# A one-core kernel for a hybrid block with experts: hx kept in SBUF through the scan, the gate in sixteen units, expert weights in 8 KB runs

## The chip, the cores and the metric

The kernel runs on one core of one Trainium2 chip. The metric is the device time in microseconds of one launch, as the median of several runs. All arithmetic is in float32.

## The reference, cut to what matters

```python
# first block: x (1, 1024, 1024), ctx (1, 256, 1024), one layer
sh_a, sc_a, g_a, sh_f, sc_f, g_f = split(silu(c) @ w_mod + b_mod, 6)
hc = ctx * (1.0 + mod_c[1]) + mod_c[0]
hx = x * (1.0 + sc_a) + sh_a
x  = layer_norm(alpha * x + g_a * latent_mixer(hx, ...), ln1_g, ln1_b)
x  = layer_norm(alpha * x + g_f * hier_moe(x * (1.0 + sc_f) + sh_f), ln2_g, ln2_b)

# latent_mixer: proj = hx @ w_in gives z, q, xbc, dt, k, v
y_f, y_b = ssd_bidirectional(xs, Bm, Cm, dt, A, hf_ctx, hb_ctx)   # chunked scan, both directions
y  = (y_f + flip(y_b) + xs * skip) * silu(z)
yg = y.reshape(L, 2, 512)                                         # two groups of 512 columns
yg = yg * rsqrt(mean(yg * yg, -1) + 1e-6)                         # a norm for each group
y_ssd = yg.reshape(L, 1024) * ssd_norm_g
# q, k: RMS norm per head, rotation; attention over 256 + 1024 keys
out = concat([y_ssd, o], -1) @ w_out

# hier_moe: 4 groups x 4 experts, 2 experts for a token; d 1024, expert width 256
gate, up = t @ w_gate[e], t @ w_up[e]
hid = silu(gate) * up * combine
y  += hid @ w_down[e]
```

A second block follows (a pooling mixer, an S5 mixer, and a feed-forward network of width 2816 made of seven half-size products). The change doesn't touch it.

## The kernel before, in words

All work is ordered by hand. Each engine has one program (a list of stage functions at the end of `build`), and semaphores tie them together; `after(eng, "ssd")` waits for all counts that end a stage. The stages of the first block are: conditions (`mod`), the modulated inputs (`hx`), the conv inputs (`xbc`), `dt`, the scan (`ssd`), the `gate`, `qkv`, the second half of the conditions (`mod2`), attention (`att`), the output product (`out`), the router and the expert slots (`moe`).

SBUF is a handful of arenas that the stages share, and `ring`, three slots of 4096 elements per partition. A panel is 1024 rows by 512 columns of a weight matrix (2 MB, in runs of 2 KB); panel j goes to slot j % 3, and `load_panels` on SP's queue waits for `panel_free[j - 3]` before it issues the load (lines 187 to 191). The panels in order are four of the conditions (0 to 3), three of xbc (4 to 6), two of z (`J_Z` = 7, 8), one of k and v (`J_KV` = 9), two of q (10, 11), then the second conditions and the output weights.

`hx`, the modulated and transposed input (8 blocks of 128 columns by 1024 tokens, 4 MB), lies in arena_b. `hc`, the same of the context (1 MB), lies in arena_t. The scan needs both places: its scratch (`xw`, `rr`, `em`, `cbm`, `tmp`, lines 216 to 221) is in arena_b, its states are over hc. So `sp_first` stores hx and hc to DRAM once they are made (lines 260, 261), the scan waits for that (`s_spill`, 32), and `sp_gate` loads them again when the scan has ended (lines 852, 853). Both z panels are loaded in the meantime.

The gate (lines 846 to 929) goes over 8 tiles of 128 tokens and two halves n of 512 columns. TensorE makes z (8 matmuls of 512 columns a unit, which the chip runs as 16 instructions), ACT takes Silu of it, VectorE multiplies it onto y, ACT squares and sums. When all 16 sums are there, one root and one reciprocal are made for all, VectorE scales the 16 pieces of y, and then TensorE transposes them, four blocks a piece, and VectorE copies each piece with its gain to `mixl`. The k, v and q products (`pe_qkv`, line 952) start after the whole gate: 10 jobs of 8 matmuls, then 8 jobs of 16, each followed by the transposes of the job before.

The experts are computed in 31 slots of 128 rows (line 1630 on). A slot's rows come from DRAM in token order of the expert (`xsl`), are transposed on TensorE (`turn`, 8 transposes, line 1648), scaled and shifted by ACT and VectorE from PSUM (`modulate`, half each, with columns of `modc`), multiplied with the gate and up weights of the slot's expert (line 1658: 8 matmuls over 512 columns, 256 of gate and 256 of up), made into hidden rows, transposed (`hidden_turn`, line 1667) and multiplied with the down weights (line 1677). TensorE's order is gate_up(s+1), hidden_turn(s), turn(s+2), down(s). The weights are double buffered. SP issues for slot s: gate and up when gate_up(s-2) has ended, then down when down(s-2) has ended; since SP's queue is in order, gate and up of slot s stand behind the wait of the down weights of slot s-1, for down(s-3). Gate and up come as `"e (k p) f -> e p k f"`, a partition reading 8 rows of 1 KB that lie 128 rows apart, down as `"e (f p) n -> e p f n"`, two rows of 4 KB. VectorE also builds tables of the second block (`dve_s5_...`) in slots 1, 3, 5, 7, 9 and 11, between `hidden_copy(s)` and `hidden(s + 1)`.

In the second block, line 1925 multiplies `hn[:, k, t:L:TC]` (TC = 8) as TensorE's weights, and line 1943 one with its weights in sequence.

Of the kernel before, what the change touches and what calls it, by code (L numbers as in the profile page):

```python
# [12 lines left out]
P = 128  # L13
D = 1024
# [63 lines left out]
def build(nc, io, out):  # L78
    ctx = ExitStack()
    with ctx:  # L80
# [25 lines left out]
        csil = sb("csil", [P, KT, 2])  # L106
        ps = ctx.enter_context(nc.psum_tensor("ps", [P, 8, HALF], F32))
# [146 lines left out]
        def sp_first(eng):  # L254
# [5 lines left out]
            eng.dma_start(hx_dram, hx.rearrange("p k n -> p (k n)")).then_inc(s_spill, 16)  # L260
# [3 lines left out]
            load_panels(eng, J_XBC + 3, J_KV)  # L264
# [350 lines left out]
        def dve_ssd(eng):  # L615
            ch = Chain(eng, steps, chained[0])
            after(eng, "xbc", "dt")
            eng.wait_ge(s_spill, 32)
# [59 lines left out]
        def pool_ssd(eng):  # L678
            after(eng, "xbc", "dt")
            eng.wait_ge(s_spill, 32)  # L680
# [36 lines left out]
        def act_ssd(eng):  # L717
            after(eng, "xbc", "dt")
            eng.wait_ge(s_spill, 32)
# [115 lines left out]
        zs = [view(arena_d, i * DSSD, DSSD) for i in range(2)]  # L835
# [3 lines left out]
        ropes = sb("ropes", [P, 2, LT, HD // 2])  # L839
# [5 lines left out]
        panel_free[J_Z] = panel_free[J_Z + 1] = (s_z, 2 * LT)  # L845

        def sp_gate(eng):
            for a in range(2):
                eng.dma_start(ropes[:, a], io["rope_table"][a].rearrange("(t p) c -> p t c", p=P)
                              ).then_inc(s_rope, 16)  # L850
            after(eng, "ssd")
            eng.dma_start(hx.rearrange("p k n -> p (k n)"), hx_dram).then_inc(s_spill, 16)
            eng.dma_start(hc.rearrange("p k n -> p (k n)"), hc_dram).then_inc(s_spill, 16)
            load_panels(eng, J_KV, NPAN1)

        def pe_gate(eng):
            after(eng, "ssd")
            eng.wait_ge(s_spill, 32 + 32)
            wait_panel(eng, J_Z)
            wait_panel(eng, J_Z + 1)  # L860
            for t in range(LT):
                for n in range(2):
                    if t >= 2:
                        eng.wait_ge(s_zs, 2 * (t - 2) + n + 1)
                    for k in range(KT):
                        mm = eng.matmul(ps[:, 2 * (t % 2) + n, :], h_tile(k, t), slot(J_Z + n)[:, k, :],  # L866
                                        start=(k == 0), stop=(k == KT - 1))
                    mm.then_inc(s_z, 1)
            eng.wait_ge(s_zn, 2 * LT)
            for t in range(LT):  # L870
                for q in range(2):
                    u = 2 * t + q
                    if u >= 4:
                        eng.wait_ge(s_zTc, u - 3)
                    for i in range(4):
                        mm = eng.transpose(ps[:, 4 + u % 4, i * P:(i + 1) * P],
                                           y[:, t, (4 * q + i) * P:(4 * q + i + 1) * P], ident[:, :])
                    mm.then_inc(s_zT, 1)

        def act_gate(eng):  # L880
            after(eng, "ssd")
            for t in range(LT):
                if t >= 2:
                    eng.wait_ge(s_zg, 2 * (t - 1))
                for n in range(2):
                    eng.wait_ge(s_z, 2 * t + n + 1)
                    eng.activation(zs[t % 2][:, n * HALF:(n + 1) * HALF], ps[:, 2 * (t % 2) + n, :], ACT.Silu
                                   ).then_inc(s_zs, 1)
# [2172 lines left out]
```

## Time and profile before

| | us |
|---|---|
| median of 3 runs | 3605.3 |
| the runs | 3598.89 to 3613.4 |
| the profiled execution | 3616.49 |
| its span (first to last instruction) | 3614.8 |
| TensorE busy | 3173.4 (88%) |
| VectorE busy | 1529.8 (42%) |
| GpSimd busy | 1051.6 (29%) |
| ACT busy | 673.3 (19%) |
| moved by DMA | 288.29 MB |

The profiled execution is one run of its own, 11 us over the median. Durations come from it. Times in the trace count from the start of its span. "PEld" is TensorE's weight load, which can overlap the matmul before it; a matmul's own duration (592 ns for 512 columns) is longer than the step from one to the next (0.43 us), since matmuls are pipelined. "issue" means that an engine waited for nothing that the profile shows.

### The profile page before, as it was taken

The page shows a single profiled execution, that of the slowest core. Times are in us where ns is not written, and L with a number is a line of the kernel's source. Part 1 is how long each engine was busy: PE and PEld are TensorE (multiplying, and loading weights), DVE is VectorE, ACT ScalarE, POOL GpSimd, SP SyncE. Part 2 cuts the span into 40 slices and gives each one's busy share as a digit, 9 for nine tenths or more (in the row PEclk, how much of TensorE's full clock was granted, in tenths as well). Part 3 has the DMA queues.
Part 4 walks back from the last instruction along what each step waited for, and adds up shares of the span by engine and source line. Part 5 has one row for each costly group of instructions (what it writes and reads, how often), then busy time and mean ns, then how long its engine had stood idle before and what let it go on. Part 6 is the DMA issues. An engine that isn't in the chain of part 4 may idle for free.

```text
span 3614.8 us, 27752 instructions
## 1 busy us (share of the span) xinstructions
PE 3173.4 (88%) x9880; PEld 1480.6 (41%) x9880; DVE 1529.8 (42%) x2447; ACT 673.3 (19%) x1440; POOL 1051.6 (29%) x953
## 2 busy tenths in 40 slices
PE   6996879898999999999758999198698999999995
PEld 3553434443333333344424444165444444444442
DVE  2335851444555555422323322616413343454345
ACT  1224631111222222300111111212201000000001
POOL 0004840000365656600010000214401355345534
PEclk8998989998999999999879999598799999999998
DMA  7000020104600000010188998300102011111101
GB/s 283 24 26 1 1 82 0 47 24 168 245 1 1 1 1 1 5 61 18 38 299 283 320 332 286 142 4 12 47 0 70 23 61 45 35 35 65 40 12 53
DMA packets 170617, 288.29 MB, mean 80 GB/s; under 512 B 22216, under 2 KB 108912, under 8 KB 169968
## 3 DMA queue, kind: packets, MB, share of 16 engines
q1 hardware_dynamic: 155632, 237.02, 19.0%
q10 hardware_dynamic: 10240, 32.71, 2.4%
q0 software_dynamic: 4608, 16.78, 1.2%
q8 instruction: 79, 1.29, 0.1%
q14 instruction: 58, 0.48, 0.0%
HBM read 236.17 MB, written 50.33 MB: 79 GB/s over the span
## 4 chain that ended last, share of the span: by engine, by line
PE 63%; issue 13%; POOL 9%; DVE 7%; DMA 6%; ACT 2%; SPq 0%; ACTq 0%; POOLq 0%; DVEq 0%
PE ps L2792 15%; PE ps L2808 6%; PE ps L1329 6%; PE ps L422 6%; PE ps L967 5%; POOL arena_b L1205 5%; PE ps L1658 5%; PE ps L2597 3%; PE ps L866 3%; DMA ring<-in_w_up 3%; PE ps L1677 2%; PE ps L1925 2%; PE ps L1943 2%; DMA ring<-in_w_mod 1%; PE ps L1107 1%
## 5 line engine op out<-in xcount | busy, mean ns | idle before, releaser
L1205 POOL TENSOR_TENSOR arena_b<-arena_b 128x512 f32<-128x512 f32 x288 | 357.6, 1268 | 298.6 <-ACT arena_b L1187 298.6
L1223 DVE TENSOR_REDUCE arena_b<-ps 128x1 f32<-128x512 f32 (+1 forms) x384 | 213.0, 597 | 245.6 <-PE ps L1107 244.4
L2764 POOL TENSOR_TENSOR arena_b<-arena_b,arena_d 128x512 f32<-128x512 f32 x132 | 165.8, 1272 | 374.4 <-DVE arena_d L2899 372.8
L1658 PE MATMUL ps<-ring,arena_a 128*128 128x512 f32 x496 | 235.5, 631 | 36.7 <-issue 16.4
L2877 DVE TENSOR_TENSOR arena_d<-arena_d,ps 128x512 f32<-128x512 f32 x154 | 101.8, 684 | 385.8 <-PE ps L2792 385.8
L1187 ACT ACTIVATE arena_b<-ps 128x512 f32<-128x512 f32 x320 | 173.7, 594 | 416.1 <-PE ps L1133 416.1
L1107 PE MATMUL ps<-arena_d,arena_a 64*128 64x512 f32 (+1 forms) x768 | 243.0, 575 | 2.3 <-DVE arena_b L1214 2.1
L1129 PE MATMUL ps<-arena_a,arena_d 64*128 64x512 f32 x640 | 218.2, 617 | 8.3 <-DVE arena_b L1243 8.3
L2896 DVE TENSOR_TENSOR arena_b<-arena_b,ps 128x512 f32<-128x512 f32 x264 | 174.6, 685 | 49.3 <-POOL arena_b L2764 25.9
L1143 PE MATMUL ps<-arena_b,arena_d 128*64 128x512 f32 x640 | 172.7, 617 | 0.0
L967 PE MATMUL ps<-ring,arena_b 128*128 128x512 f32 x384 | 169.1, 597 | 1.7 <-DVE arena_c L924 1.7
L1658 PEld LDWEIGHTS ps<-ring,arena_a 128*128 128x128 f32 x496 | 98.7, 202 | 169.7 <-issue 144.9
L422 PE MATMUL ps<-arena_b,ring 128*128 128x512 f32 x384 | 166.9, 592 | 0.8 <-ACT arena_b L401 0.8
L1107 PEld LDWEIGHTS ps<-arena_d,arena_a 64*128 64x128 f32 x768 | 86.0, 189 | 182.9 <-issue 119.0
L2792 PE MATMUL ps<-arena_a,ring 128*128 128x512 f32 x352 | 154.7, 598 | 1.3 <-DVE arena_a L1882 1.3
L1615 POOL DMA_INDIRECT arena_d<-yslots,arena_t x8 | 7.6, 945 | 448.4 <-DMA yslots<-arena_a 442.3
L687 POOL TENSOR_TENSOR arena_b<-m_le,arena_t 128x512 f32<-128x512 f32 x32 | 40.4, 1262 | 315.6 <-DVE arena_t L558 310.2
L2808 PE MATMUL ps<-arena_c,arena_t 128*128 128x512 f32 x264 | 128.2, 594 | 0.0
L866 PE MATMUL ps<-ring,arena_b 128*128 128x512 f32 x256 | 111.8, 599 | 15.7 <-DMA arena_t<-hc_dram 15.7
L1398 PE MATMUL ps<-ident,arena_t 128*128 128x128 f32 x128 | 26.5, 379 | 100.4 <-ACT arena_t L1821 84.3
L1677 PE MATMUL ps<-ring,arena_c 128*128 128x512 f32 x248 | 111.7, 593 | 2.0 <-DVE arena_c L1753 1.5
L1329 PE MATMUL ps<-ring,arena_c 128*128 128x512 f32 x256 | 113.2, 595 | 0.0
(504 smaller groups left out, 5006.4 us busy)
## 6 DMA issues: line engine op xcount, KB each, us to landing
ring<-in_w_gate SPq DMA_DIRECT2D x42, 1024.0 KB, 7.6
ring<-in_w_up SPq DMA_DIRECT2D x42, 1024.0 KB, 10.8
ring<-in_w_down SPq DMA_DIRECT2D x42, 1024.0 KB, 5.5
ring<-in_w_mod SPq DMA_DIRECT2D x12, 2048.0 KB, 13.3
ring<-in_w_in SPq DMA_DIRECT2D x10, 2048.0 KB, 13.2
xslots<-arena_c SPq DMA_DIRECT2D x1, 15872.0 KB, 52.1
arena_a<-xslots ACTq DMA_DIRECT2D x31, 512.0 KB, 5.6
yslots<-arena_a ACTq DMA_DIRECT2D x31, 512.0 KB, 5.4
```

What stands on the lines that cost most here:

```text
L422: mm = eng.matmul(ps[:, b, 0:n], w[:, k, (m % 4) * P:(m % 4 + 1) * P], src[:, k, :], start=(k == 0), stop=(k == KT - 1))
L866: mm = eng.matmul(ps[:, 2 * (t % 2) + n, :], h_tile(k, t), slot(J_Z + n)[:, k, :], start=(k == 0), stop=(k == KT - 1))
L967: mm = eng.matmul(ps[:, 2 * (j % 2) + n, :], h_tile(k, t), w[:, k, :], start=(k == 0), stop=(k == KT - 1))
L1107: eng.matmul(ps[:, u % 3, 0:k1 - k0], qT[rows, pr, q0:q0 + P], kT[rows, pr // 2, k0:k1], start=True, stop=True).then_inc(s_S, 1)
L1129: eng.matmul(ps[:, 4 + e, :], kT[rows, pr // 2, kt * P:(kt + 1) * P], qT[rows, pr, qs], start=True, stop=False)
L1205: eng.tensor_tensor(acc, first, prT[n % NPR], ALU.add).then_inc(s_pa, 1)
L1223: eng.tensor_reduce(mx3[j % 2][:, t, e, piece:piece + 1], ps[:, u % 3, 0:k1 - k0], AX.X, ALU.max).then_inc(s_mx, 1)
L1329: mm = eng.matmul(ps[:, u % 3, :], (mixl if k < KT else mixu)[:, k % KT, t * P:(t + 1) * P], w[:, k % KT, :], start=(k == 0), stop=(k == 2 ...
L1658: mm = eng.matmul(ps[:, s % 2, :], xsT[s % 2][:, k, :], sguw[s % 2][:, k, :], start=(k == 0), stop=(k == KT - 1))
L1677: mm = eng.matmul(ps[:, 5 + h, :], hTs[s % 2][:, f, :], sdnw[s % 2][:, f, h * HALF:(h + 1) * HALF], start=(f == 0), stop=(f == 1))
L2792: mm = eng.matmul(bank_of("gu", b, w, p), lhs, rhs, start=(k == 0), stop=(k == HK - 1))
L2808: eng.matmul(bank_of("dn", b, i, p), lhs[p], rhs[p], start=True, stop=True).then_inc(dn_done, 1)
```

## The change

1. hx stays in arena_b through the scan. The scan's scratch moves to the ring: `uu` and `rr` to slot 0, `xw`, `em` and `cbm` to slot 2; the two `tmp` rows go to the free end of arena_d and into the buffer of the rope tables. Only the first z panel (slot 1) is loaded before the scan. The second, hc and the rope tables are loaded after it. hc is still stored and loaded again.
2. The gate runs as 16 units, half n = 0 of all tiles first. Each unit has its own sum, root and reciprocal, and is transposed two units later, between the z products. The first k/v product is issued ahead of the last transposes.
3. The expert weights are read so that a partition takes 8 adjacent rows of gate and of up (8 KB in one run) and 2 adjacent rows of down (8 KB). The contraction index of block k is then p * 8 + k instead of k * 128 + p. So the transposes of the slot's rows read every 8th column, those of the hidden rows every 2nd, and the shift and scale come from a new table `modp` in that order, made by a trip of the 16 columns through DRAM behind `mod2`.

```diff
-        xw = view(arena_b, 0, 2, DSSD)
-        rr = view(arena_b, 2048, 2, 2, HALF)
-        em = view(arena_b, 4096, 2, HALF)
-        uu = view(ring, 0, 2, 2, HALF)
-        cbm = view(arena_b, 6144, 2, 2, 2 * NST)
-        tmp = [view(arena_b, 7168 + i * HALF, HALF) for i in range(2)]
-        hx_dram = nc.dram_tensor("hx_dram", [P, KT * L], F32).ap()
+        uu, rr = view(ring, 0, 2, 2, HALF), view(ring, 4 * HALF, 2, 2, HALF)
+        xw = view(ring, 2 * PAN, 2, DSSD)
+        em = view(ring, 2 * PAN + 4 * HALF, 2, HALF)
+        cbm = view(ring, 2 * PAN + 6 * HALF, 2, 2, 2 * NST)
+        tmp = [view(arena_d, 4 * (L + CTX) + NT * 2 * NST, HALF),
+               ropes[:, :, :, :].rearrange("p a t c -> p (a t c)")]
...
-            eng.dma_start(hx_dram, hx.rearrange("p k n -> p (k n)")).then_inc(s_spill, 16)
-            load_panels(eng, J_XBC + 3, J_KV)
+            load_panels(eng, J_XBC + 3, J_Z + 1)
...
         def sp_gate(eng):
+            after(eng, "ssd")
+            load_panels(eng, J_Z + 1, J_KV)
+            eng.dma_start(hc.rearrange("p k n -> p (k n)"), hc_dram).then_inc(s_spill, 16)
             for a in range(2):
                 eng.dma_start(ropes[:, a], io["rope_table"][a].rearrange("(t p) c -> p t c", p=P)
                               ).then_inc(s_rope, 16)
-            after(eng, "ssd")
-            eng.dma_start(hx.rearrange("p k n -> p (k n)"), hx_dram).then_inc(s_spill, 16)
-            eng.dma_start(hc.rearrange("p k n -> p (k n)"), hc_dram).then_inc(s_spill, 16)
             load_panels(eng, J_KV, NPAN1)
...
+            for u, (n, t) in enumerate(ZUNITS):      # pe_gate
+                if t == 0:
+                    wait_panel(eng, J_Z + n)
+                if u >= 4:
+                    eng.wait_ge(s_zs, u - 3)
+                for k in range(KT):
+                    mm = eng.matmul(ps[:, u % 4, :], hx[:, k, t * P:(t + 1) * P], slot(J_Z + n)[:, k, :],
+                                    start=(k == 0), stop=(k == KT - 1))
+                mm.then_inc(s_z, 1)
+                if u >= 2:
+                    turn(u - 2)
+            turn(2 * LT - 2)
+            pe_qkv_product(eng, 0)
+            turn(2 * LT - 1)
...
+            for u, (n, t) in enumerate(ZUNITS):      # act_gate
+                eng.wait_ge(s_z, u + 1)
+                if u >= 4:
+                    eng.wait_ge(s_zg, u - 3)
+                eng.activation(zs[u % 4], ps[:, u % 4, :], ACT.Silu).then_inc(s_zs, 1)
                 eng.wait_ge(s_zg, u + 1)
+                    eng.wait_ge(s_zss, 2 * u)
                 eng.activation(sqz, y[:, t, n * HALF:(n + 1) * HALF], ACT.Square,
                                accum_out=ssum[:, u:u + 1]).then_inc(s_zss, 1)
+                eng.wait_ge(s_zq, 2 * u + 1)
+                eng.activation(rst[:, u:u + 1], ssum[:, u:u + 1], ACT.Sqrt).then_inc(s_zss, 1)
...
+        modp = csil.rearrange("p k v -> p (k v)").rearrange("p (v k) -> p v k", v=2)
+        def sp_mod_columns(eng):                     # SP: behind sp_zero, ahead of sp_out
+            after(eng, "mod2")
+            eng.dma_start(mod_dram.rearrange("(n p) -> p n", p=P), modc[:, 3 * KT:5 * KT, 0],
+                          allow_slow_non_contiguous=True).then_inc(s_rope, 16)
+            eng.wait_ge(s_rope, 32 + 16)
+            eng.dma_start(modp, mod_dram.rearrange("(v p k) -> p v k", v=2, k=KT)).then_inc(s_rope, 16)
...
-            gate_of = io["w_gate"][0].rearrange("e (k p) f -> e p k f", p=P)
-            down_of = io["w_down"][0].rearrange("e (f p) n -> e p f n", p=P)
+            gate_of = io["w_gate"][0].rearrange("e (p k) f -> e p k f", p=P)
+            down_of = io["w_down"][0].rearrange("e (p f) n -> e p f n", p=P)
-                eng.dma_start(sguw[s % 2][:, :, 0:FE], gate_of[e]).then_inc(gu_in[s % 2], 16)
-                eng.dma_start(sguw[s % 2][:, :, FE:], up_of[e]).then_inc(gu_in[s % 2], 16)
+                eng.dma_start(sguw[s % 2][:, 0], gate_of[e]).then_inc(gu_in[s % 2], 16)
+                eng.dma_start(sguw[s % 2][:, 1], up_of[e]).then_inc(gu_in[s % 2], 16)
...
-                                       xsl[s % 3][:, k * P:(k + 1) * P], ident[:, :])
+                                       xsl[s % 3].rearrange("p (c k) -> p k c", k=KT)[:, k, :], ident[:, :])
-                    mm = eng.matmul(ps[:, s % 2, :], xsT[s % 2][:, k, :], sguw[s % 2][:, k, :],
+                    mm = eng.matmul(ps[:, s % 2, :], xsT[s % 2][:, k, :], sguw[s % 2][:, :, k, :],
-                    mm = eng.transpose(ps[:, 4, f * P:(f + 1) * P], hds[s % 2][:, f * P:(f + 1) * P], ident[:, :])
+                    mm = eng.transpose(ps[:, 4, f * P:(f + 1) * P], hds[s % 2].rearrange("p (c f) -> p f c", f=2)[:, f, :], ident[:, :])
```

## Rows read from the trace of the kernel before

**Rows 1.** The page: busy tenths of TensorE and DMA in 40 slices of 90 us.
```profile
PE   6996879898999999999758999198698999999995
DMA  7000020104600000010188998300102011111101
```
**Rows 2.** The chain of waits, 500 to 700 us: start us, us, what.
```profile
515.19 0.70 DVE arena_a L635
...
516.29 14.24 DMA arena_t<-hc_dram
...
530.88 111.78 PE ps L866 x256
...
666.98 15.70 PE ps L967 x32
...
683.12 6.87 PE ps L967 x16
```
**Rows 3.** The timeline of ACT at the gate's end: start us, us, what.
```profile
642.69 0.60 ACT L887 ACTIVATE arena_d<-ps 128x512 f32<-128x512 f32 x1 [6.21 <-PE ps L866]
643.18 0.62 ACT L901 ACTIVATE arena_d<-arena_a 128x512 f32<-128x512 f32 x1
...
643.99 0.63 ACT L901 ACTIVATE arena_d<-arena_a 128x512 f32<-128x512 f32 x1
...
646.35 1.28 ACT L893 ACT_TABLE_LOAD   x1
```
**Rows 4.** The timeline of VectorE, gate's end and first k row.
```profile
643.32 0.69 DVE L909 TENSOR_TENSOR arena_a<-arena_a,arena_d 128x512 f32<-128x512 f32 x1 [6.12 <-ACT arena_d L887]
...
680.15 0.43 DVE L1050 COPY arena_c<-arena_t 128x512 f32<-128x512 f32 x1
```
**Rows 5.** TensorE's groups, 1847 to 2256 us: busy us, mean ns, idle before.
```profile
L1658 PE MATMUL ps<-ring,arena_a 128*128 128x512 f32 x496 | 235.5, 631 | 36.7 <-issue 16.4 <-DMA ring<-in_w_up 16.2 <-ACT arena_a L1708 4.1
```
**Rows 6.** The timeline of TensorE in the slots: start us, us, what.
```profile
1963.48 0.38 PE L1667 MATMUL ps<-ident,arena_a 128*128 128x128 f32 x2
1963.70 1.04 PE L1648 MATMUL ps<-ident,arena_a 128*128 128x128 f32 x8
1964.57 3.60 PE L1677 MATMUL ps<-ring,arena_c 128*128 128x512 f32 x8
1972.52 9.86 PE L1658 MATMUL ps<-ring,arena_a 128*128 128x512 f32 x16 [4.36 <-issue]
```
**Rows 7.** The timeline of VectorE ahead of the gate/up product at 1972.5.
```profile
1971.06 1.36 DVE L1739 TENSOR_SCALAR arena_a<-ps,modc 128x128 f32<-128x128 f32 x4
```
**Rows 8.** The chain of waits, 2035 to 2068 us.
```profile
2038.09 3.45 PE ps L1677 x8
...
2043.17 11.71 DMA ring<-in_w_up
```
**Rows 9.** Line 1637, which loads w_up: its 31 DMAs.
```profile
DMA to landing us min/median/max: 9.3/11.1/32.9
```
**Rows 10.** Windows: us, PE, PEld, DVE, ACT, POOL busy, PEclk, DMA share, GB/s.
```profile
1972.00:1980.00 8.00, 7.48 (x11) 3.29 (x12) 1.55 (x3) 0.00 (x0) 0.00 (x0) 0.62 0.89 300
...
1805.00:1843.00 38.00, 0.00 (x0) 0.00 (x0) 10.91 (x49) 1.86 (x4) 15.44 (x16) 0.50 1.04 403
```
**Rows 11.** GB/s in 40 slices: runs of 1 KB (2829:2843), 2 KB (2572:2582), 4 KB (3479:3488).
```profile
GB/s 0 0 0 0 0 0 79 102 219 304 372 383 395 383 383 369 360 342 351 354 348 342 348 336 193 26 0 0 0 0 0 0 0 0 0 0 0 0 0 0
GB/s 0 0 0 0 0 131 156 180 352 336 401 410 401 401 393 377 393 418 410 410 401 418 418 401 401 401 393 336 49 0 0 0 0 0 0 0 0 0 0 0
GB/s 0 0 0 0 127 18 309 146 182 255 400 437 400 437 400 400 419 400 310 18 0 0 0 0 0 0 0 0 0 0 0 0 0 0 0 0 0 0 0 0
```
**Rows 12.** Weight loads of lines 1925 and 1943: ns min/median/max, first and last start.
```profile
L1925 PEld LDWEIGHTS ps<-ring,arena_a x128: 312/313/334, 2358.1 to 2412.4; 128*128 128x128 f32 x128
L1943 PEld LDWEIGHTS ps<-arena_a,ring x128: 190/190/192, 2412.8 to 2473.4; 128*128 128x128 f32 x128
```
**Rows 13.** The timeline of TensorE, 301.7 to 304.5 us.
```profile
301.81 2.42 PE L522 MATMUL ps<-sel,arena_a 128*128 128x32 f32 x20 [1.61 <-DVE arena_a L538]
```

More of the change, by code:

```diff
@@ L834, in build @@
         mixl = view(arena_c, 0, KT, L)
-        zs = [view(arena_d, i * DSSD, DSSD) for i in range(2)]
+        zs = [view(arena_d, i * HALF, HALF) for i in range(4)]
         sqz = view(arena_d, 2 * DSSD, HALF)
@@ L857, in pe_gate @@
             after(eng, "ssd")
[L858 to L878, printed above, removed]
+            def turn(u):
+                n, t = ZUNITS[u]
+                eng.wait_ge(s_zn, u + 1)
+                if u >= 4:
+                    eng.wait_ge(s_zTc, u - 3)
+                for i in range(4):
+                    mm = eng.transpose(ps[:, 4 + u % 4, i * P:(i + 1) * P],
+                                       y[:, t, (4 * n + i) * P:(4 * n + i + 1) * P], ident[:, :])
+                mm.then_inc(s_zT, 1)
@@ L880, in act_gate @@
+            turn(2 * LT - 2)
+            pe_qkv_product(eng, 0)
+            turn(2 * LT - 1)
         def act_gate(eng):
             after(eng, "ssd")
[L882 to L888, printed above, removed]
-                if t >= 1:
-                    gate_squares(eng, t - 1)
@@ L891, in act_gate @@
-            gate_squares(eng, LT - 1)
-            eng.wait_ge(s_zq, 1)
-            eng.activation(rst, ssum, ACT.Sqrt).then_inc(s_silu, 1)
-        def gate_squares(eng, t):
-            for n in range(2):
-                u = 2 * t + n
+            for u, (n, t) in enumerate(ZUNITS):
+                eng.wait_ge(s_z, u + 1)
+                if u >= 4:
+                    eng.wait_ge(s_zg, u - 3)
+                eng.activation(zs[u % 4], ps[:, u % 4, :], ACT.Silu).then_inc(s_zs, 1)
                 eng.wait_ge(s_zg, u + 1)
@@ new lines, in dve_gate @@
+            for u, (n, t) in enumerate(ZUNITS):
+                v = y[:, t, n * HALF:(n + 1) * HALF]
+                r = rst[:, u:u + 1]
+                eng.wait_ge(s_zs, u + 1)
+                eng.tensor_tensor(v, v, zs[u % 4], ALU.mult).then_inc(s_zg, 1)
+                if u >= 3:
+                    turned_gate(u - 3)
+                eng.wait_ge(s_zss, 2 * u + 1)
+                step(eng, eng.tensor_scalar(ssum[:, u:u + 1], ssum[:, u:u + 1], 1.0 / HALF, EPS_RMS,
+                                            ALU.mult, ALU.add), s_zq, 2 * u + 1)
+                eng.wait_ge(s_zss, 2 * u + 2)
+                step(eng, eng.reciprocal(r, r), s_zq, 2 * u + 2)
+                eng.tensor_scalar(v, v, r, None, ALU.mult).then_inc(s_zn, 1)
@@ L932, in build @@
+            for u in range(2 * LT - 3, 2 * LT):
+                turned_gate(u)
+        ends["gate"] = [(s_zTc, 2 * LT), (s_zq, 4 * LT), (s_zs, 2 * LT), (s_zss, 4 * LT)]
         kT = view(arena_d, 0, KVH, L + CTX)
@@ L950, in build, with pe_qkv_product @@
         panel_free[J_Q] = panel_free[J_Q + 1] = (s_qkp, NJ)
+        def pe_qkv_product(eng, j):
+            kind, t = JOBS[j]
+            if j == 0:
+                wait_panel(eng, J_KV)
+            if j == LT:
+                eng.wait_ge(s_spill, 16 + 16)
+            if j == NT:
+                wait_panel(eng, J_Q)
+                wait_panel(eng, J_Q + 1)
+            if j < 2:
+                eng.wait_ge(s_zs, 2 * LT - 2 + 2 * j)
+            else:
+                eng.wait_ge(s_qkn, j - 1)
+                eng.wait_ge(s_qkv, min(j - 1, NT))
+            for n in range(2 if kind == "q" else 1):
+                w = slot(J_Q + n) if kind == "q" else slot(J_KV)
+                for k in range(KT):
+                    mm = eng.matmul(ps[:, 2 * (j % 2) + n, :], h_tile(k, t), w[:, k, :],
+                                    start=(k == 0), stop=(k == KT - 1))
+            mm.then_inc(s_qkp, 1)
@@ L1586, in build @@
         BS = KT * 2 * FE + 2 * D
-        sguw = [view(ring, i * BS, KT, 2 * FE) for i in range(2)]
+        sguw = [view(ring, i * BS, 2, KT, FE) for i in range(2)]
         sdnw = [view(ring, i * BS + KT * 2 * FE, 2, D) for i in range(2)]
```

102 lines of the change are left out of this document (38 added, 64 removed).

## The prediction, made before the changed kernel was run

> **What bounds the kernel now.** I began with the page: TensorE works 88% of the span and is at 9 tenths or more of a slice nearly everywhere except around slices 6 and 7 (about 515 to 670 us) and 19 to 25 (1780 to 2300 us); DMA is near idle except in the second of these, around attention's end and at the start [rows 1]. So two stretches matter: the end of the scan with the gate behind it, and the expert slots.
>
> For the first I read the chain of waits [rows 2]. VectorE's last addition of the scan ends at 515.9, hx and hc come back from DRAM until 530.5, the 256 z matmuls (16 units of 16) take 111.8, and then a serial tail (squares, root, 16 scalings of y, 64 transposes with their copies) runs until the first k/v product at 667.0. In steady state a product takes 6.87 and 0.44 for its four transposes, without a gap (the first two end at 682.68, the next starts at 683.12). The tail is 667.0 - 642.7 = 24.3 us.
>
> For the slots I read TensorE's groups, then its timeline. Gate/up waited 36.7 us in all: 16.4 in five slots put down to "issue", 16.2 in six for w_up, 4.1 at the start for ACT [rows 5]. A slot without a wait is gate/up 6.87 (16 matmuls, as a k/v product), hidden turn 0.22, turn of x 0.87, down 3.44: 11.4 us [rows 6]. 31 of them are 353; the stretch from 1847 to 2256 has 409. The five are slots where VectorE works through s5 tables before the next hidden and modulated rows: its scaling of rows ends at 1972.4 and gate/up starts at 1972.5 [rows 6, 7]. That gate/up takes 9.86, where 16 such matmuls take 6.87 otherwise; the granted clock there is 0.62 of full [rows 6, 10]. The loads set the rest: a slot's weights are issued when the down product of three slots earlier ends, here at 2041.5, and w_up lands at 2054.9, 13.3 later, against a slot of 11.4 [rows 8]. From its own issue it takes at least 9.3 and 11.1 in the median [rows 9].
>
> **Gate.** (1) The hx reload goes: z can start at 516.1. The second z panel (2 MB) is now loaded there and needed at unit 8, 58 us on; hc and the rope tables ride behind it, needed after 640. All of that is under 4 MB, and the 5 MB of before landed in 14.2 us [rows 2]. (2) A unit becomes 6.87 + 0.44 = 7.31, the step that the k/v products already show: 16 units are 117.0. The first k/v product is issued ahead of the last turn, so the second starts at 516.1 + 117.0 + 6.9 = 640.0. Before, it starts at 682.7 - 6.9 = 675.8. Gain 35.8.
>
> What could take it back is the chain through ACT and VectorE, now serial per unit, with Silu's and Sqrt's tables alternating. By the rows [rows 3, 4]: Silu 0.63 to the multiply, multiply 0.69, Square with its accumulator read 0.81, mean 0.2, table load 1.28, the root of one column 0.3 by the size of such small steps, table load for the next Silu 1.28: 5.2 us per unit against 7.31. Both loads are counted in full, so nothing comes on top if they queue behind a wait. The cover is 2.1 us; without it each missing us costs 16. The last unit's chain (5.5 with reciprocal and scaling) lies under the turn before it and a product (7.3), and the first k row's chain (675.8 to VectorE's copy ending at 680.6, 4.8, plus 0.9 for the gate's last copy) under the second product [rows 4]. The idle 15 us before z and the tail each left a slow start (15.70 for two products instead of 13.74), which the smaller seams may keep or lose: +2 or -1. So 33.8 to 36.8, and I take 35.6.
>
> **Scan.** Its buffers move (xw, rr, em, masks to the ring, two scratch rows elsewhere); instructions, shapes and types stay. No row shows that an address matters. The 4 MB store of hx also goes; it is issued when hx is made, and the scan, which waits for it, comes only after all conv products. Nothing, +-1.
>
> **Expert weights.** (3) Gate and up come in 8 KB runs instead of 1, down in 8 instead of 4. Of three loads that run alone, 1 KB runs settle at 342 to 354 GB/s, 2 KB runs at 401 to 418, 4 KB at 400 to 437 [rows 11]. There is no 8 KB row; the nearest is 4 KB, so I take 410 (bounds 345 and 435). The 2.1 MB then take 5.1 instead of 6.0 us. All DMA work of a slot, 3.1 MB of weights and 1.05 MB of rows in and out, is 10.2 us at 410 and 12.0 at 350. (4) The rows' columns must follow the weights' new order, so the turn of x reads `xsl` at a stride of 8 elements as TensorE's weights. The trace has this access: L1925 loads `hn[:, k, t:L:TC]`, TC = 8, in 313 ns, beside 190 for the same shape in sequence in L1943 [rows 12]. There it hid under 512-column matmuls. In a turn it can't: eight turns in 0.87 are one per 0.109, and L522's 20 matmuls of 32 columns keep 0.113 too [rows 6, 13], so the pace is that of the weight loads. Plus 0.123 each, 0.98 per slot. Bounds: nothing, and 0.327 each if a strided load ran at a quarter of that pace. The hidden turn has stride 2 and no row; 0 to 0.25 per slot, and I take 0, as half of each piece read is still used.
>
> The Trainium skill ("SBUF — State Buffer", "Door 1: The DMA port swizzle") speaks against (4): accesses that each go to a new 16-byte line pay a penalty, and two hits per line are enough for full bandwidth. The trace agrees for the stride of 8 and gives the size [rows 12]; of the stride of 2 no run here shows anything yet. By that rule the sum would stay as it is.
>
> (5) A slot becomes 12.4. In the five slots bound by VectorE the longer turn lies inside the wait (2.6 to 4.4), so 26 x 0.98 = +25.5. The waits for w_up go: the work of 10.2 is under 12.4, and w_up lands 13.3 less 0.9 and less the backlog, about 11 behind the down product. That is 16.2 and the slow clock behind them, at most 3 each as at 1972.5 and less behind shorter waits; I take 4 for the six: -20 (bounds -14, if some come back, and -22). The start of the stage, 1805 to 1843, is all DMA at 403 GB/s [rows 10], 4.2 MB of it in 1 KB runs: -1.5 (0 to -2). The waits for VectorE stay.
>
> (6) The shift and scale columns go to DRAM and back in 4-byte pieces. Both DMAs and SP's wait for mod2, which ends ahead of attention, stand behind the zero fill and ahead of the out stage's loads, which wait for attention (1533) anyway; the columns are needed at 1843. Attention covers them by 600 us. Nothing. The new waits of ACT and VectorE in the slots are fulfilled long before.
>
> **Sum.** -35.6 + 25.5 - 20 - 1.5 = -31.6. The profiled execution (3616.5) goes to 3585, the median of the runs (3605.3, 11 lower) to 3574. Half a percent, about what a measurement of this kernel can tell from no change, is 18 us: faster is under 3587.
>
> **Rivals.** A, the strided turn is free, because loads overlap deeper in a turn than under a matmul. The +25.5 goes away, the slot stays 11.4 and some short waits for w_up return (+3): 3551. For it: loads of 190 ns keep a pace of 0.11 as well as those of 140. Against: 123 ns more for the same 128 columns look like time of reading. Chance 0.13.
> B, run length brings nothing in the mix of queues and 350 GB/s remains. Then 12.0 of work meets a slot of 12.4, w_up lands about 12.7 behind and 0.3 late in 24 slots, and the start gains nothing: +9, 3583. For it: beside POOL's queue 403 GB/s is reached with 1 KB runs in the mix [rows 10]. Chance 0.14.
> The Trainium skill ("DMA: Bandwidth & Descriptors", "Specifications") backs B: from 512 bytes on a transfer runs at line rate. By that rule 1 KB runs lose nothing; the rates of the loads alone, 350 beside 405, speak against it [rows 11].
> C, a gate unit's chain is longer than TensorE's 7.31, say 8.3 with VectorE's copies in the way: +16, 3590. Against: 5.2 by the rows. Chance 0.06.
> D, slower than before: strided loads at a quarter pace in both turns. Ten per slot at 0.327 are 3.3 us, in 26 slots +85 instead of +25.5: 3633. It decides from 0.22 per load on (57 us of gains / 26 / 10). Against: 0.123 by L1925. Chance 0.05.
> That the change doesn't do what it says would be a gap at 516 as before; the reload of hx is out of the code, so that gets no chance of its own. The forecast keeps 0.62.
>
> **Numbers.** 3574 by the forecast case, whose own bounds give 3560 to 3588. The range of 3550 to 3593 takes in A, B and C; D is left out. The forecast case lies nearly whole under 3587, A wholly, B for the most part, C hardly: faster 0.85, same 0.10, slower 0.05.
>
> **What the profile after should show.** z within 1 us of the scan's end; a step of 7.3 in the gate; the second k/v product at 640; ACT idle some 2 us per unit. Loads of the x turn near 260 ns, eight turns in 1.85 us; slots of 12.4 with no wait for w_up; the five s5 waits 1 us shorter, their gate/up starting as late behind the hidden turn as now. I am wrong if turns still take 0.87 (A), if w_up is waited for by more than a few us in all (B), if gate steps are over 7.5 (C), or if turns take over 3 us (D).

## The result, and the profile after

| | before | after |
|---|---|---|
| median, run side by side | 3605.56 us (4 runs) | 3569.59 us (4 runs, 3567.2 to 3576.23) |
| ratio | | 0.9894, 95% interval 0.9878 to 0.991 |
| the profiled execution, its span | 3616.49, 3614.8 | 3567.2, 3565.5 |
| TensorE busy | 3173.4 (88%) | 3159.0 (89%) |
| ACT busy | 673.3 | 715.2 |
| moved by DMA | 288.29 MB | 279.93 MB |

The median falls by 36.0 us, to 4 under the forecast of 3574. The two profiled executions differ by 49.3, because that of before was 11 over its median and that of after 2 under it.

The page after the change, against [rows 1]: a slice is now 89 us. The holes at the end of the scan and in the slots are narrower, but the second is still there (slices 19 to 25).

```profile
PE   6996889997999999999668997297698999999995
...
DMA  6000010107300000100378897100102021112101
```

The chain of waits after, 509 to 645 us, against [rows 2]: start us, us, what.

```profile
509.71 0.70 DVE arena_a L634
510.41 0.04 issue
510.45 23.20 PE ps L874 x48
533.65 0.44 PE ps L864 x4
534.09 6.87 PE ps L874 x16
540.96 0.44 PE ps L864 x4
541.40 6.87 PE ps L874 x16
...
628.63 0.87 PE ps L864 x8
629.50 6.87 PE ps L963 x16
636.37 0.44 PE ps L864 x4
636.81 6.87 PE ps L963 x16
```

No DMA stands between the scan and z. From the end of the scan (510.4) to the second k/v product (636.8) are 126.4 us, where before there were 159.9 (515.9 to 675.8): 33.5 less. A step is 7.31 (534.09 to 541.40), as forecast. Only the start is slow: the first three units take 23.2 for what later takes 20.6. Two windows of that stretch say why (us, PE, PEld, DVE, ACT, POOL busy, PEclk, DMA share, GB/s):

```profile
510.50:515.00 4.50, 4.50 (x6) 1.92 (x7) 0.00 (x0) 0.00 (x0) 0.00 (x0) 0.50 0.77 245
515.00:534.00 19.00, 19.00 (x49) 8.66 (x48) 2.99 (x8) 9.76 (x14) 0.00 (x0) 1.00 0.69 232
```

z starts at a granted clock of 0.50, the lower level of 1.2 GHz, and is at 1.00, 2.4 GHz, in the window from 515 on. The clock fell ahead of z: it is 1.00 from 503 to 508 and 0.61 from 508.0 to 509.7, where the scan's last eight small products run behind 1.75 us without work.

The timeline of ACT in a gate unit, against [rows 3]:

```profile
595.75 1.28 ACT L889 ACT_TABLE_LOAD   x1
599.45 0.60 ACT L889 ACTIVATE arena_d<-ps 128x512 f32<-128x512 f32 x1 [2.41 <-PE ps L874]
600.80 0.63 ACT L893 ACTIVATE arena_d<-arena_a 128x512 f32<-128x512 f32 x1 [0.76 <-DVE arena_a L911]
601.34 0.19 ACT L893 ACTIVATION_READ_ACCUMULATOR arena_d<-arena_a 128x1 f32 x1
601.54 1.28 ACT L896 ACT_TABLE_LOAD   x1
602.84 0.20 ACT L896 ACTIVATE arena_d<-arena_d 128x1 f32<-128x1 f32 x1
603.05 1.28 ACT L889 ACT_TABLE_LOAD   x1
```

ACT waits 2.41 us per unit for TensorE, so its chain stays under the product; the table load for the next Silu (595.75) is made ahead of that wait, not behind it.

TensorE in the slots after, as its group, then a plain stretch of its timeline, against [rows 5, 6]:

```profile
L1671 PE MATMUL ps<-ring,arena_a 128*128 128x512 f32 x496 | 231.1, 621 | 28.7 <-issue 17.4 <-DMA ring<-in_w_up 7.2 <-ACT arena_a L1721 4.1
```

```profile
1998.42 7.03 PE L1671 MATMUL ps<-ring,arena_a 128*128 128x512 f32 x16
2005.29 0.39 PE L1680 MATMUL ps<-ident,arena_a 128*128 128x128 f32 x2
2005.51 1.06 PE L1661 MATMUL ps<-ident,arena_a 128*128 128x128 f32 x8
2006.41 3.60 PE L1690 MATMUL ps<-ring,arena_c 128*128 128x512 f32 x8
2009.85 7.03 PE L1671 MATMUL ps<-ring,arena_a 128*128 128x512 f32 x16
```

A slot without a wait takes 11.43 (1998.42 to 2009.85), as before, not 12.4: the strided turn costs 0.90 (2005.51 to 2006.41) where the plain one cost 0.87. The waits for w_up are 7.2 us instead of 16.2, not gone. Those of VectorE (issue, 17.4) are there as they were.

By stage the difference between the two profiled executions (-49.3) is: scan end -5.5, gate -33.5, start of the slots (scatter to first turn) +0.8, first turn to the end of the last down product -11.6 (413.4 to 401.9), the rest within 0.5. The -5.5 isn't the change's: the conv products, whose code is the same, start at 57.2 here and at 60.6 there, and the scan's end goes with that start. The kernel before, profiled once more (`e4` below), starts them at 57.2 too and ends its scan at 510.7, beside 510.4 here; this kernel, profiled once more (`e5`), starts them at 60.9 and ends its scan at 516.9.

### The profile page after: what moved, and what is told of

Same layout as the page of the kernel before. It is cut to its first block, busy times and chain, and to the rows that moved or that the text cites. A ratio compares the mean times of both kernels' runs of the same rounds, so it can differ in the third digit from the quotient of the medians.

```text
span 3565.5 us, 27860 instructions
## 1 busy us (share of the span) xinstructions
PE 3159.0 (89%) x9880; PEld 1471.4 (41%) x9880; DVE 1535.9 (43%) x2477; ACT 715.2 (20%) x1485; POOL 1051.1 (29%) x953
## 2 busy tenths in 40 slices
DMA packets 113147, 279.93 MB, mean 79 GB/s; under 512 B 24520, under 2 KB 47728, under 8 KB 100848
## 4 chain that ended last, share of the span: by engine, by line
PE 65%; issue 13%; POOL 9%; DVE 7%; DMA 4%; ACT 1%; ACTq 0%; SPq 0%; POOLq 0%; DVEq 0%
PE ps L2807 15%; PE ps L2823 6%; PE ps L1331 6%; PE ps L421 6%; PE ps L1671 5%; PE ps L963 5%; POOL arena_b L1207 5%; PE ps L874 3%; PE ps L2612 3%; PE ps L1690 2%; DMA ring<-in_w_up 2%; PE ps L1940 2%; PE ps L1958 2%; DMA ring<-in_w_mod 1%; PE ps L1109 1%
## 5 line engine op out<-in xcount | busy, mean ns | idle before, releaser
L1671 PE MATMUL ps<-ring,arena_a 128*128 128x512 f32 x496 | 231.1, 621 | 28.7 <-issue 17.4
L686 POOL TENSOR_TENSOR ring<-m_le,arena_t 128x512 f32<-128x512 f32 x32 | 40.4, 1262 | 309.7 <-DVE arena_t L557 306.0
```

Of the source, the lines that this page charges most:

```text
L1671: mm = eng.matmul(ps[:, s % 2, :], xsT[s % 2][:, k, :], sguw[s % 2][:, :, k, :], start=(k == 0), stop=(k == KT - 1))
```

## The experiments

In all kernels the time from the start of the first gate/up product to the start of the last matmul of the last down product is called the slot stretch. It is 409.0 us in the profile of before, 397.3 in that of after. The ratios of each table are to the kernel before, run beside the kernels of that table; that is why its median differs from table to table.

### Each half of the change alone

`e1_gate_part` is the changed kernel with the expert part undone. `e2_weights_part` is the kernel before with the expert part alone. `e3_hx_reloaded` is the changed kernel with the store and reload of hx back in. `e4_before_again` is the kernel before, profiled once more.

e1 against the changed kernel (e2 has the same lines the other way, against the kernel before):

```diff
-            gate_of = io["w_gate"][0].rearrange("e (p k) f -> e p k f", p=P)
+            gate_of = io["w_gate"][0].rearrange("e (k p) f -> e p k f", p=P)
...
-                                       xsl[s % 3].rearrange("p (c k) -> p k c", k=KT)[:, k, :], ident[:, :])
+                                       xsl[s % 3][:, k * P:(k + 1) * P], ident[:, :])
```

e3 against the changed kernel:

```diff
+            eng.dma_start(hx_dram, hx.rearrange("p k n -> p (k n)")).then_inc(s_spill, 16)
...
+            eng.dma_start(hx.rearrange("p k n -> p (k n)"), hx_dram).then_inc(s_spill, 16)
```

Besides, hc's reload goes ahead of the second z panel again, and z waits for both reloads, as in the kernel before.

> The change without its expert weights: hx kept, gate in units, weights and row turns of the slots as before. Theory (the two parts are independent, gate worth 33.5 us by the traces): 3605.6 - 33.5 = 3572, ratio 0.9907; w_up waited for as often as before (about 16 us). Rival (the profiled pair differs by 49 us because the gate part is worth more than its stage, through a shift of later stages): under 3562.

> The expert weights alone on the kernel before: 8 KB runs, strided turns, the table of shifts in the new order. Theory (the traces give 413.4 to 401.9 us for the slots): -11.6, so 3594, ratio 0.9968. Rival (what the blind sum said: turns 0.98 us longer, loads hidden): +4, ratio 1.001. Rival (the medians moved by 36, the gate took 33.5 of it, so the weights are worth only 2.5): ratio 0.9993.

> The changed kernel with hx stored and reloaded as before, everything else kept (gate in units, last panel behind the reloads). Theory (the reload is the gap of 14.2 to 15 us ahead of z, of which a slow start of 1 us comes back): +14, so 3584 against 3569.6 of the change, ratio to before 0.9939. Rival (the gate in units hides part of the reload): under +5.

> The kernel before once more, for its profile alone. Theory (the first profiled execution was 11 us over the median by chance, in the waits for w_up and in the start): a span nearer 3603, the slots shorter than 413 us or the start shorter. Rival (profiling adds it always): a span near 3615 again.

Measured, against a median of 3610.69 for the kernel before (19 runs, 3597 to 3624):

| kernel | median us | ratio (95%) | z starts | slot stretch | waits for w_up | issue |
|---|---|---|---|---|---|---|
| e1, gate part | 3581.28 | 0.9924 (0.9897 to 0.995) | 516.7 | 405.9 | 12.5 | 16.3 |
| e2, weights part | 3604.62 | 0.9981 (0.9962 to 1.0) | 530.7 | 398.6 | 7.5 | 16.2 |
| e3, hx reloaded | 3589.53 | 0.9942 (0.9923 to 0.9961) | 527.0 | 397.2 | 7.4 | 17.4 |
| e4, before again | 3608.14 (one run) | | 525.8 | 403.3 | 9.8 | 16.3 |

The chain of waits of e3 behind the scan:

```profile
511.17 0.70 DVE arena_a L636
512.27 14.49 DMA arena_t<-hc_dram
527.00 18.07 PE ps L878 x38
...
652.52 6.87 PE ps L967 x16
```

The gate part brings 27 us by its ratio (18 to 37 by the interval; 33.5 by the trace), the weights part 7 (0 to 14). Their product, 0.9905, lies in the interval of the whole (0.9878 to 0.991). e1's median of 3581 is 9 over what was expected of it, with an interval that takes in the expected 0.9907; its slots waited 12.5 us for w_up.

By the traces hx in SBUF is a little less than half of the gate part. With the reloads ahead of z again, z starts 15.1 us behind VectorE's last addition instead of 0.04. From the scan's end (511.9) to the second k/v product (652.5) e3 takes 140.6 us, where the changed kernel takes 126.4 and the one before 159.9. So the reloads are 14.2 of the 33.5 and the gate in units is 19.3. The medians give the reloads more: e3 is 18 to 20 us slower than the changed kernel (3571.61 and 3569.59 in its two sets of runs), where 14 was expected. Of the 18.3 between the two profiles, 2.5 lie between the k/v products and the first slot. There two executions of the changed kernel itself (after and e5) differ by 3.1, so this part isn't shown to be the reload's.

e4 shows what one profile hides. Its w_up waits are 9.8 us and its slot stretch 403.3, where the first profile of the same kernel had 16.2 and 409.0. The old weights give 409.0, 403.3 and 405.9 (mean 406.1); the new ones, in five profiles (after, e2, e3, e5, e6), 397.2 to 398.6 (mean 397.7). So the weights part is worth 8.4 us, and some 3 of the 11.6 between the two profiles were the draw of one execution.

### The strided turn and the run length

`e5_change_again` is the changed kernel unaltered. `e6_plain_turns` reads the rows in sequence in both turns. `e7_short_runs` brings the weights in runs of 1 and 4 KB again and leaves all else. In both, the rows' columns no longer stand in the order of the weight rows, so that the expert products multiply other pairs.

e6 against the changed kernel (it is the same in the hidden turn), then e7:

```diff
-                                       xsl[s % 3].rearrange("p (c k) -> p k c", k=KT)[:, k, :], ident[:, :])
+                                       xsl[s % 3][:, k * P:(k + 1) * P], ident[:, :])
```

```diff
-            gate_of = io["w_gate"][0].rearrange("e (p k) f -> e p k f", p=P)
-            up_of = io["w_up"][0].rearrange("e (p k) f -> e p k f", p=P)
-            down_of = io["w_down"][0].rearrange("e (p f) n -> e p f n", p=P)
+            gate_of = io["w_gate"][0].rearrange("e (k p) f -> e p k f", p=P)
+            up_of = io["w_up"][0].rearrange("e (k p) f -> e p k f", p=P)
+            down_of = io["w_down"][0].rearrange("e (f p) n -> e p f n", p=P)
```

> The changed kernel again, as the base for the other kernels of this row. Theory (gate -34 by the traces, weights -8 as the mean of three profiles each way): ratio 0.988 to 0.990, slots of 397 to 399 us, six VectorE-bound waits of 16 to 18 us in all, w_up waited for 7 to 8.

> The changed kernel with the turns of x and of the hidden rows read in sequence again; this leaves the columns in another order than the weights' rows, so values differ. Theory (a strided turn costs only 0.02 us, rival A of the prediction): loads 140 instead of 193 ns, no difference in time, under 1 us. Rival (the strided turn holds something back that the turn's own time does not show, e.g. the row scaling or the DMA writes into SBUF): 5 us or more faster, slots under 393 us.

> The changed kernel with its expert weights in 1 and 4 KB runs again, turns strided; the rows of the weights are then in another order than the columns, so values differ. Theory (the gain of the weights part is run length alone): slots back to 403 to 409 us, w_up waited for 10 to 16 us, +8 on the change. Rival (the gain came from the new place or order in SBUF): slots stay at 397 to 399.

Measured, against a median of 3612.14 for the kernel before (7 runs):

| kernel | median us | ratio (95%) | slot stretch | w_up | issue |
|---|---|---|---|---|---|
| e5, change again | 3571.61 | 0.988 (0.9863 to 0.9896) | 397.9 | 7.5 | 17.4 |
| e6, plain turns | 3569.12 | 0.9877 (0.9861 to 0.9894) | 397.3 | 7.3 | 16.3 |
| e7, short runs | 3579.17 | 0.9908 (0.989 to 0.9926) | 405.3 | 15.4 | 13.6 |

The x turn's weight loads, after and in e6, then those of the hidden turn after (ns min/median/max):

```profile
L1661 PEld LDWEIGHTS ps<-ident,arena_a x248: 186/193/226, 1805.1 to 2186.5; 128*128 128x128 f32 x124
```

```profile
L1661 PEld LDWEIGHTS ps<-ident,arena_a x248: 139/140/230, 1805.7 to 2187.1; 128*128 128x128 f32 x124
```

```profile
L1680 PEld LDWEIGHTS ps<-ident,arena_a x62: 194/196/199, 1827.2 to 2201.5; 128*128 128x128 f32 x62
```

The strided load of a transposition takes 193 ns instead of 140, and the kernel doesn't feel it: e5 and e6 have the same time within their intervals and the same stretch within 0.6 us. That is rival A's outcome. A stride of 2 costs the load as much as one of 8: 196 ns, where e6 has 141. The shorter runs cost 8 us by the medians (3579.17 beside 3571.61, with intervals that just overlap), and the slots show it more clearly (405.3 beside 397.9; no profile with long runs is over 398.6), with the waits for w_up back at 15.4. The stretch 1835 to 2195 of after, then of e7, shows the same load on the queues at another price:

```profile
1835.00:2195.00 360.00, 335.39 (x958) 163.01 (x957) 118.86 (x315) 52.83 (x140) 0.00 (x0) 0.97 0.85 324
```

```profile
1835.00:2195.00 360.00, 331.00 (x941) 160.86 (x940) 116.26 (x310) 51.48 (x136) 0.00 (x0) 0.96 0.92 318
```

The DMA engines are busy 0.85 of the time for 324 GB/s, and 0.92 for 318: per byte 10% more with short runs. So run length matters and rival B falls. Whether gate and up (1 KB) or down (4 KB) bring the most wasn't told apart.

### When does a strided load cost its time?

The prediction priced the turn by a strided load of the second block (313 ns). `e8_matmul_turns` makes the x turn of the changed kernel a plain float32 product with the identity, which the chip runs as 16 instructions, with the same strided rows. `e12_matmul_in_seq` is e8 with rows in sequence; as in e6, other pairs are multiplied.

```diff
-                    mm = eng.transpose(ps[:, 2 + k // 4, (k % 4) * P:(k % 4 + 1) * P],
-                                       xsl[s % 3].rearrange("p (c k) -> p k c", k=KT)[:, k, :], ident[:, :])
+                    mm = eng.matmul(ps[:, 2 + k // 4, (k % 4) * P:(k % 4 + 1) * P],
+                                    xsl[s % 3].rearrange("p (c k) -> p k c", k=KT)[:, k, :], ident[:, :],
+                                    start=True, stop=True)
```

> The changed kernel with the turn of x done as a plain float32 product with the identity (two instructions a block) instead of a transposition. It measures the strided load as in the second block's product with hn. Theory (there a strided load reads at half pace, 313 ns, while a transposition's load is another, shorter form): loads of 313 ns and one instruction per 0.23 us, a turn of 3.7 us, slots 2.8 us longer. Rival (load time beyond the pace is latency that overlaps in either form): one per 0.11 us, a turn of 1.8 us, slots 0.9 us longer.

> The kernel of e8_matmul_turns (the x turn as a plain float32 product with the identity, 16 instructions), but with rows read in sequence instead of at a stride of 8; this makes the columns of the rows stand in another order than the weight rows, which changes that part of the computation. e8's turns hold loads of 335 ns and one instruction per 0.237 us, 3.79 to the next operation. If the stride is what costs in the plain float32 form, and only there, loads are 190 ns, as in the second block's line with weights in sequence, and the pace falls to 0.11 to 0.12: the turn takes 1.9 and the stage of 31 slots 451 - 31 x 1.9 + some waits for w_up = 395 to 405. Rival: the plain form itself is slow at 128 columns, stride or not: pace 0.237 as before, stage 451.

The timeline of TensorE in e8, then in e12:

```profile
2014.04 3.96 PE L1661 MATMUL ps<-ident,arena_a 128*128 128x128 f32 x16
2017.83 3.60 PE L1691 MATMUL ps<-ring,arena_c 128*128 128x512 f32 x8
```

```profile
2011.63 1.95 PE L1661 MATMUL ps<-ident,arena_a 128*128 128x128 f32 x16
2013.42 3.60 PE L1691 MATMUL ps<-ring,arena_c 128*128 128x512 f32 x8
```

Turn to down product is 3.79 us with strided rows, 1.79 in sequence: 0.237 and 0.112 per instruction, with loads of 335 and 192 ns. So the +0.125 is real in a plain float32 product, and there it comes with the stride alone. In a transposition the stride adds 53 ns to the load and 0.004 to the pace (0.112 beside 0.109). The single runs were 3629.72 (e8, stretch 451.2) and 3579.67 (e12, stretch 403.8). They show a second thing: with a slot of 14.3 the waits for w_up are gone, with 12.3 they are 1.7 us. The waits put down to issue fell too, to 2.4 and 12.0: a longer slot gives VectorE more time.

### What still holds the slots

The chain of waits after, in a slot that waits for w_up, against [rows 8]:

```profile
2029.43 3.45 PE ps L1690 x8
2032.89 0.33 SPq L1653
...
2033.98 1.27 SPq L1649
...
2035.35 10.58 DMA ring<-in_w_up
2045.93 0.04 issue
2045.97 7.13 PE ps L1671 x16
```

The down product's end releases SP, which issues down, gate and up in this order. w_up lands at 2045.93, 13.1 behind the product; in the next slot 11.9 (2057.69 to 2069.63). The landing alone is 10.6 and 10.4 here, and 10.0 to 12.2 in all six slots where w_up ends the chain, beside 10.9 to 13.9 in nine such slots of before [rows 8]. `e9_loads_ahead` lets SP issue gate and up ahead of the wait for the down buffer; `e10_tables_behind` moves VectorE's s5 tables behind the rows that TensorE waits for; `e11_both` does both.

e9:

```diff
-                if s >= 2:
-                    eng.wait_ge(dn_done, s - 1)
-                eng.dma_start(sdnw[s % 2], down_of[e]).then_inc(dn_in[s % 2], 16)
+                if s >= 1:
+                    down_load(s - 1)
...
+            down_load(NSLOT - 1)
```

Here `down_load(s)` holds the three removed lines for slot s. In e10 these lines of VectorE's program now stand ahead of the slot's `dve_s5_...` calls, not behind them:

```python
                 if s + 1 < NSLOT:
                     hidden(s + 1)
                 if s + 2 < NSLOT:
                     modulate(s + 2)
                 store(s)
```

> The changed kernel, with SP issuing gate and up of slot s before it waits to issue down of slot s-1; nothing else moved. If the waits for w_up that are left (7 to 9 us in the changed kernel and its repetition) come from SP standing in front of the down load while gate and up could go already, they go away: the ratio to the kernel before falls from 0.989 to 0.987, about 3562, and the stage of 31 slots from 398 us to 390. The waits put down to issue (17.4), which are VectorE's, stay. Rival: the weights' buffers are free only when their product ends, so that an earlier issue starts no earlier or meets the rows of x and y in the queues: no change, 3570.

> The changed kernel, with VectorE's s5 table work of a slot moved behind the hidden rows, the modulated rows and the store of the same slot. If the waits put down to issue are VectorE standing in the s5 tables before the rows that TensorE waits for, they go (17.4 us), with the slow clock behind them (up to 3 in each of six slots, of which I count 1 each): 20 us less, 3550, ratio 0.983, the stage 378 us. Rival: the slots without a wait run into the loads and waits for w_up grow from 7 to 15 or more, as with short runs: 12 us less or under, 3558.

> Both moves at once, in the changed kernel. If VectorE's tables and SP's order are all that holds the slots above 11.43 us, the stage of 31 slots is 31 x 11.43 + 6 = 360 us instead of 398, and the kernel 3535, ratio 0.979. Rival: the loads themselves are the bound by then (10 us of DMA work per slot, with the landing 10 to 12 after the issue), and waits for w_up of 10 us or more are left: 3550, ratio 0.983.

Measured, against a median of 3611.46 for the kernel before (7 runs):

| kernel | median us | ratio (95%) | slot stretch | w_up | issue |
|---|---|---|---|---|---|
| e9, loads ahead | 3558.93 | 0.9853 (0.9826 to 0.988) | 387.9 | 0 | 17.4 |
| e10, tables behind | 3548.37 | 0.9817 (0.9785 to 0.9849) | 375.1 | 11.9 | 0 |
| e11, both | 3534.4 | 0.9785 (0.9758 to 0.9812) | 360.8 | 0 | 0 |

TensorE's group in e10, then in e11:

```profile
L1671 PE MATMUL ps<-ring,arena_a 128*128 128x512 f32 x496 | 221.1, 599 | 16.1 <-DMA ring<-in_w_up 11.9 <-ACT arena_a L1721 4.1
```

```profile
L1677 PE MATMUL ps<-ring,arena_a 128*128 128x512 f32 x496 | 220.7, 598 | 4.1 <-ACT arena_a L1727 4.1
```

Each move takes away the wait it aims at, and the waits of the other kind stay or grow (7.2 to 11.9 in e10). The slow clock goes with VectorE's waits: behind one of them, from 1985.2 to 1990.0, the changed kernel has a granted clock of 0.64, and gate/up is busy 231.1 in it and 221.1 in e10, whose clock from 1835 to 2155 is 1.00. The stretch lost 17.4 of waits and these 10.0 (6 were counted), and got back 4.7 of waits for w_up: 22.7, about what it shows (397.3 to 375.1), where 20 was expected. With both moves the stretch is 360.8, as expected 360, and the loads are still not the bound at 11.4 us per slot, though the DMA engines are busy 0.92 of the time from 1835 to 2155. e11 is 35 us under the changed kernel (37 under e5) and 77 under the one before.

## Why the prediction was right, and where its steps were not

The range held and the gate's mechanism came as forecast, but that the time was met to 4 us is in part luck. The two largest terms of the slots were both wrong: the 25.5 us of the strided turn didn't come, and the waits for w_up gave back 11.6 less than forecast. The two errors partly cancelled.

**Gate (1, 2): forecast -35.6, measured -33.5.** The reload's place, the step of 7.31 and the cover of about 2 us on ACT came as forecast, and rival C falls. ACT's chain is 4.9 us per unit (599.45 to 604.33) where 5.2 was counted. From the scan's end to the second k/v product the forecast was 123.9 us (516.1 to 640.0) and the trace has 126.4. Nearly all of the 2.5 is the first z products at clock 0.50. The prediction had this as "+2 or -1" at the seams and took 0.2. The chain of waits in e11, at the start and the end of the gate:

```profile
515.13 0.04 issue
...
631.01 0.87 PE ps L864 x8
631.89 6.87 PE ps L963 x16
638.76 0.44 PE ps L864 x4
639.19 3.01 PE ps L963 x7
```

From 515.1 to 639.2 are 124.1, the forecast. A window of its first z products has the granted clock at 1.00:

```profile
515.30:519.80 4.50, 4.50 (x11) 2.07 (x12) 0.00 (x0) 0.00 (x0) 0.00 (x0) 1.00 0.78 246
```

The code up to there is that of the changed kernel. In e11 the clock is 1.00 in the scan's last eight products too (513.3 to 514.4), where after it had fallen. Three executions (e10, e11, e12) have no slow z product, the longest being 0.70 us; seven (after, e1, e5 to e9) have one of 1.22. Why, stays open. All three had a late start of the conv products (60.3 to 61.0), but so had e1 and e5.

**Scan: forecast nothing, +-1, and so it came.** From the first conv product to the scan's end, executions that start these products at 56.9 to 57.8 take 453.5 with the old buffers (e4) and 453.2 to 453.6 with the new ones (after, e6 to e9), with 454.4 in e3. Those that start at 60.3 to 61.0 take 455.3 and 455.0 with the old (before, e2) and 454.9 to 456.0 with the new (e1, e5, e10 to e12). The 2 us go with the start, not with the buffers. Why there are two starts is open.

**Strided turn (4, 5): forecast +25.5, measured nothing (0.03 us a slot in the timeline, none in e6).** This is the step that failed. The load of `L1925` (313 ns) is that of a plain float32 product, the turn's that of a transposition. The same stride of 8 costs 0.125 us per instruction in the one form, as computed, and 0.004 in the other. The price went wrong with the row that it was taken from. Rival A, with 0.13, named the outcome but not the reason: a load as long as that row's isn't hidden in a turn either (335 ns in e8, pace 0.237); the transposition's is a shorter one. Its time of 3551 was 18 us too low, because it too let nearly all waits for w_up go. By the prediction's own sign (turns that still take 0.87; they took 0.90) the forecast case was wrong here. What misled me was "the pace is that of the weight loads": before, loads of 140 ns and of 190 ns had the same pace of 0.11 [rows 6, 13], which already said that a load up to 190 is hidden. 193 was just inside, 335 far outside; no run has a load between them in a turn.

The Trainium skill ("SBUF — State Buffer", "Door 1: The DMA port swizzle") says that accesses to a new 16-byte line each pay a penalty and that two hits per line are enough for full bandwidth. At the stride of 8 the loads agree in direction, 193 beside 140 ns in transpositions and 335 beside 192 in plain products. At the stride of 2, which takes two float32 elements from each such line, the trace doesn't agree: 196 beside 141 ns, as much as at 8. That a longer load can be hidden whole is shown by e6.

**Waits for w_up: forecast -20, measured about -8.** This term hung on the wrong one: it let them go because a slot would be 12.4 long. With a slot of 11.43 and w_up landing 11.9 and 13.1 behind the down product in the two slots shown (forecast: about 11), 7.2 are left. Where a slot was 12.3 long (e12) they did fall to 1.7, so the rule behind the step held. Besides, the 16.2 of [rows 5] was a high draw; e4 and e1 had 9.8 and 12.5 with the same weights, and e7 15.4 with the same run lengths. "More than a few us in all" was also the prediction's sign for rival B; 7.2 are there and B is still wrong, so it was a poor sign. The measured 8 is the change of the slot stretch: about 5 of it are waits, the rest is gate/up's own busy time (235.5 to 236.6 us with the old weights; 231.0 to 233.1 with the new).

**Run length (3): 5.1 instead of 6.0 us, rival B.** Rival B falls with e7: run length is worth 8 us. Per byte the short runs take 10% more DMA time (0.92 at 318 GB/s, 0.85 at 324), where the prediction's 12.0 and 10.2 us per slot are 18% more. The gain shows in the waits for w_up and the slow stretches behind them; nothing came at the start of the slots.

**Start of the slots: forecast -1.5, measured +0.8** in the first pair of executions. From the last k/v/q matmul to the first gate/up product are 990.9, 991.3, 993.9 and 990.9 us with short runs (before, e4, e1, e7), and 991.6, 991.5, 994.1, 994.7 and 991.6 with long ones (after, e2, e3, e5, e6; 992.2, 993.5 and 991.7 in e9 to e11). So no gain shows, but with 3 us between executions one of 1.5 could be hidden. The cause wasn't tested.

**Waits for VectorE: forecast unchanged in the sum, measured 16.4 before and 17.4 after.** The 1 us by which each was to shrink was the longer turn's, which didn't come. And (6), the columns through DRAM, shows nowhere: the stages from the second half of the conditions to the scatter are all shifted by 39.1 to 39.5.

With the terms as measured the sum is -33.5 + 0 - 8.4 + 0.8 = -41 against the forecast -31.6; the medians say -36.0 beside the first runs and -40.5 in e5's (3612.14 to 3571.61). By the traces the sum is thus 9.5 off, and how near the median came is in part the draw of the runs. Had the strided turn cost its 25.5, and the 7.2 of waits gone with it, the kernel would stand at about 3588, at the edge of what can be told from no change.

## What to carry to other kernels

Price a strided or otherwise odd operand by a row of the same instruction form, and look at the pace from one instruction to the next, not at the duration of the load: what the pipeline hides costs nothing until it sticks out. Terms that hang on one another (here a longer slot and the waits that it would hide) must be changed together in every case that is worked out. And in a loop with little slack, look at what an in-order queue or engine does ahead of the item that is waited for: two moves of lines, with no less work, were worth 35 us, about as much as the whole change. A size that rests on waits for loads wants more than one profile of each kernel.

## What was not expected of the hardware

A transposition's strided weight load (193 ns) ran at a pace of 0.112 us per instruction, a plain float32 product's (335 ns) at 0.237. The granted clock at the start of z was 0.50 in some executions and 1.00 in others of the same code, worth 2.3 us (118.8 and 116.5 to the first k/v product). And two profiles of one kernel had waits for w_up of 16.2 and 9.8 us, and a slot stretch of 409.0 and 403.3.
